# The last output projection by seven products of half-size blocks, in two units

## What is computed

```python
o = o * jax.nn.silu(z)                  # attention output, gated: 256 x 1024
x = x + gate_row * (o @ w_out_odd)      # w_out_odd: 1024 x 1024; gate_row comes from the condition
return rms_norm(x, final_g)             # 256 x 1024
```

## Time and profile before

| what | value |
|---|---|
| median of 3 runs | 1536.67 us (1536.63 to 1539.48) |
| the profiled execution | 1536.52 us, of which 1534.7 us are the span of the profile |
| TensorE busy | 1515.6 us, 99% of the span |
| VectorE, ScalarE, GpSimd busy | 1036.0, 431.0 and 12.3 us |
| granted TensorE clock, mean | 0.998 of full speed |

### The profile page before, as it was taken

How to read it: one execution, slowest core, us unless ns; L and a number is a source line. 1 busy time by engine, 2 the same in 40 slices (tenths; PEclk the granted TensorE clock), 3 DMA queues, 4 the chain that set the end, 5 groups by cost and what they waited for, 6 DMA issues and landing times.

```text
span 1534.7 us, 27707 instructions
## 1 busy us (share of the span) xinstructions
PE 1515.6 (99%) x11119; PEld 1344.5 (88%) x11119; DVE 1036.0 (68%) x1942; ACT 431.0 (28%) x925; POOL 12.3 (1%) x26
## 2 busy tenths in 40 slices
PE   8999999999999999999999999999999999999998
PEld 7998869898899999899878899799999787678887
DVE  5788886477667774678897467667775564536663
ACT  5415424012100001335423201300011365424432
POOL 1000000000000000100000000000000000000000
PEclk9999999999999999999999999999999999999999
DMA  8543453353465445344242442485454746373420
GB/s 278 185 165 111 150 153 111 111 198 131 148 237 165 153 169 178 119 163 154 101 157 92 165 142 97 146 274 165 159 179 159 245 163 220 111 289 121 141 109 28
DMA packets 176993, 243.42 MB, mean 159 GB/s; under 512 B 21438, under 2 KB 99940, under 8 KB 176868
## 3 DMA queue, kind: packets, MB, share of 16 engines
q1 hardware_dynamic: 174980, 237.98, 45.3%
q10 hardware_dynamic: 1888, 3.67, 0.7%
HBM read 240.56 MB, written 1.05 MB: 157 GB/s over the span
## 4 chain that ended last, share of the span: by engine, by line
PE 95%; DVE 2%; DMA 1%; ACT 1%; issue 0%; ACTq 0%; DVEq 0%; SPq 0%
PE psum L630 34%; PE psum L1657 27%; PE psum L1512 7%; PE psum L1312 3%; PE psum L3125 3%; PE psum L445 2%; PE psum L1571 2%; PE psum L3225 2%; PE psum L1307 2%; PE psum L3217 2%; PE psum L428 2%; PE psum L1441 1%; PE psum L1564 1%; PE psum L461 1%; PE psum L1413 1%; PE psum L1352 1%
## 5 line engine op out<-in xcount | busy, mean ns | idle before, releaser
L630 PE MATMUL psum<-hT,ring 128*128 128x256 f32 x1552 | 342.8, 380 | 0.9 <-ACT hT L3322 0.7
L630 PEld LDWEIGHTS psum<-hT,ring 128*128 128x128 f32 x1552 | 292.3, 190 | 45.4 <-issue 6.9
L630 PE MATMUL psum<-uT,ring 128*128 128x256 f32 x384 | 84.9, 380 | 0.0
L1657 PE MATMUL psum<-hT,ring 128*128 128x128 f32 x704 | 82.3, 275 | 0.0
L630 PEld LDWEIGHTS psum<-uT,ring 128*128 128x128 f32 x384 | 72.6, 190 | 10.4 <-DVE uT L1175 0.6
L1657 PEld LDWEIGHTS psum<-hT,ring 128*128 128x128 f32 x704 | 80.5, 192 | 0.0
L1938 ACT ACTIVATE SCR<-SCR 128x512 f32<-128x512 f32 x22 | 13.9, 630 | 220.2 <-DVEq L2723 220.2
L491 ACT ACTIVATE SCR<-psum,stats 128x128 f32<-128x128 f32 (+2 forms) x128 | 49.7, 405 | 26.1 <-DVE stats L526 25.3
L512 DVE TENSOR_TENSOR psum<-psum,const 128x512 f32<-128x512 f32 (+4 forms) x41 | 22.1, 559 | 43.4 <-PE psum L445 42.5
L1657 PE MATMUL psum<-G,ring 128*128 128x128 f32 x400 | 47.8, 276 | 0.0
L477 ACT ACTIVATE SCR<-psum 128x512 f32<-128x512 f32 (+2 forms) x60 | 26.3, 497 | 71.6 <-PE psum L461 71.6
(11 more groups left out here) (658 smaller groups left out, 3004.0 us busy)
## 6 DMA issues: line engine op xcount, KB each, us to landing
ring<-in_w_in SPq DMA_DIRECT2D x46, 1024.0 KB, 7.0
ring<-in_ffn_w_gate_up SPq DMA_DIRECT2D x88, 512.0 KB, 5.6
ring<-in_w_ada SPq DMA_DIRECT2D x24, 1024.0 KB, 7.7
ring<-in_ffn_w_down SPq DMA_DIRECT2D x16, 1024.0 KB, 6.0
ring<-in_w_in_odd SPq DMA_DIRECT2D x16, 1024.0 KB, 7.9
ring<-in_w_in_even SPq DMA_DIRECT2D x10, 1024.0 KB, 7.1
ring<-in_x_w_kv SPq DMA_DIRECT2D x8, 1024.0 KB, 5.9
ring<-in_ssm_w_glu SPq DMA_DIRECT2D x8, 1024.0 KB, 6.5
```

The lines of the kernel that those rows point to most:

```text
L630: ins = nc.tensor.matmul(b[0:width, n * S:n * S + S], w[k // 4][:, k % 4, c0[n]:c0[n] + width], tile(k), start=k == 0, stop=k == kt - 1)
L1657: ins = nc.tensor.matmul(banks[job][:, at:at + P], left, right, start=first, stop=last)
```

## The change

The last projection is made by seven products of blocks, in two units of 512 output channels (unit 0: tiles 0 to 3, unit 1: tiles 4 to 7). `odd_out(u, p)` does product p of unit u as 8 matmuls of 128x128. The products need token differences (four, shared by both units; VectorE, `odd_tokens`), sums of weight blocks for unit 0 (four, VectorE, `odd_weights`) and for unit 1 (four, GpSimd, the new block). The first three products fill steps 8 and 9 of the attention; the other eleven follow behind its last step in the order of `OUT_LATE`. GpSimd starts when Z1's last job is full (its sums are read no more) and VectorE has normalised the last rows. VectorE makes sum 0 and difference 0 at the head of step 8, sum 1 in step 9, the rest behind the last step.

`odd_store` combines the products in `whole` and adds two tiles at a time into `xT` (`odd_added`). ScalarE copies product 1 of each unit into `one` and squares four tiles of unit 0 and twice two of unit 1. The gains come four, two and two at a time. The sums of squares take five passes on TensorE (tiles 0 with 1 to 3 added in, 5, 7, 4, 6) where there were two.

```diff
-          8: ["part 0", "part 1"], 9: ["part 2"]}
+          8: ["part 0 1", "part 0 5"], 9: ["part 1 1"]}
...
-ODD_TILES = EVEN_TILES[0:3] + [slice(6, 7), slice(7, 8)]
+OUT_JOBS = [(0, "a"), (1, "a"), (0, "b"), (0, "c"), (0, "d"), (1, "b"), (1, "c"), (1, "d")]
+OUT_LATE = [(1, 5), (0, 2), (1, 2), (0, 6), (0, 7), (0, 4), (0, 3), (1, 6), (1, 7), (1, 4), (1, 3)]
...
-    names += [f"odd out{c}" for c in range(5)] + [f"final{n}" for n in range(4)]
+    names += [f"O{u} {job}" for u, job in OUT_JOBS] + [f"final{n}" for n in range(4)]
...
-        wide(f"odd out{n}", a["w_out_odd_2"], 512 * n, 512, f"odd out{(1, 4)[n]}")
+        wide(f"odd out{n}", a["w_out_odd_2"], 512 * n, 512, f"O{n} d")
...
+    odd_sums = [[QKr[:, 1024 * i:1024 * i + 1024].rearrange("p (k g n) -> p k g n", g=2, n=P) for i in range(4)], sums]
+    def odd_quarters(eng, u):
+        w = [ring.arrived(eng, f"odd out{u}.{h}").rearrange("p k (g m n) -> p k g m n", g=2, m=2) for h in range(2)]
+        return [[w[half][:, :, :, m_, :] for half in range(2)] for m_ in range(2)]
...
+    @block.gpsimd
+    def _(pool):
+        jobs.full(pool, f"{SEVENS[-1]} d")
+        pool.wait_ge(rows_ready, att_c.base + len(C_UNITS))
+        q, made = odd_quarters(pool, 1), odd_sums[1]
+        nc.gpsimd.tensor_tensor(made[0], q[1][0], q[1][1], ALU.add).then_inc(sig["pool_mixed"], 1)
+        pool.wait_ge(sig["pool_mixed"], 1)
+        nc.gpsimd.tensor_tensor(made[1], made[0], q[0][0], ALU.subtract).then_inc(sig["pool_mixed"], 1)
+        nc.gpsimd.tensor_tensor(made[2], q[0][0], q[1][0], ALU.subtract).then_inc(sig["pool_mixed"], 1)
+        pool.wait_ge(sig["pool_mixed"], 3)
+        nc.gpsimd.tensor_tensor(made[3], q[0][1], made[1], ALU.subtract).then_inc(sig["pool_mixed"], 1)
     @block.tensor
...
+        def odd_out(u, p):
+            job = next(x for x, made in PRODUCTS.items() if p in made)
+            i, name = PRODUCTS[job].index(p), f"O{u} {job}"
+            first = p in (1, 5) or job in "cd" and i == 0
+            if first:
+                out_banks[name] = jobs.begin(pe, name, early=p in (1, 5))
+            b = out_banks[name]
+            w = [ring.arrived(pe, f"odd out{u}.{h}") for h in range(2)]
+            if p in MIXED_OF:
+                pe.wait_ge(sig["tokens_mixed"], 4 + MIXED_OF[p] + 1)
+            if p in SUM_OF:
+                if u:
+                    pe.wait_ge(sig["pool_mixed"], SUM_OF[p] + 1)
+                else:
+                    pe.wait_ge(sig["weights_mixed"], 4 * len(SEVENS) + SUM_OF[p] + 1)
+            for g in range(2):
+                for k in range(4):
+                    if p in TOKENS_OF:
+                        half, n = TOKENS_OF[p]
+                        if g == 0:
+                            odd_tile(4 * half + k)
+                        tokens = z[:, 4 * half + k, n * P:(n + 1) * P]
+                    else:
+                        tokens = mixed[MIXED_OF[p]][:, k, :]
+                    if p in WEIGHTS_OF:
+                        m_, half = WEIGHTS_OF[p]
+                        weights = w[half][:, k, 256 * g + P * m_:256 * g + P * m_ + P]
+                    else:
+                        weights = odd_sums[u][SUM_OF[p]][:, k, g, :]
+                    at = S * i + P * g
+                    ins = nc.tensor.matmul(b[:, at:at + P], weights, tokens, start=k == 0, stop=k == 3)
+            if p in (2, 6, 4, 3):
+                close(ins)
...
                 if name.startswith("part"):
-                    out_part("odd", int(name[-1]), range(4), odd_tile)
+                    odd_out(int(name[5]), int(name[7]))
...
-        finish("odd", 4, odd_tile)
         def final(n):
...
-                pe.wait_ge(sig["gained_out"], (1, 1, 2, 2, 3, 3, 4, 5)[4 * half + i])
+                pe.wait_ge(sig["gained_out"], (1, 1, 1, 1, 3, 2, 3, 2)[4 * half + i])
...
-        for c, c0 in zip((3, 4), pair(3)):
-            transposed(f"odd out{c}", wide("odd out1"), (c0,), z, KT, (P,))
+        for u, p in OUT_LATE:
+            odd_out(u, p)
...
         b = ojobs.begin(pe, "square 3")
-        pe.wait_ge(sig["summed"], 4)
-        for k in (0, 7):
+        pe.wait_ge(sig["summed"], 3)
+        for k in (0, 5, 7, 4, 6):
...
-                pe.wait_ge(sig["squares"], 13)
+                pe.wait_ge(sig["squares"], 10 if k % 2 else 11)
...
-                                       start=k == t == 0, stop=k == 7 and t == 1)
+                                       start=k == t == 0, stop=k == 6 and t == 1)
...
         def square(n):
...
-            for c, tiles in enumerate(EVEN_TILES if n == 2 else ODD_TILES):
-                jobs.evacuated(act, f"{'even' if n == 2 else 'odd'} out{c}")
-                nc.scalar.activation(sq[:, tiles, :], xT[:, tiles, :], ACT.Square).then_inc(sig["squares"], 1)
+            if n == 2:
+                for c, tiles in enumerate(EVEN_TILES):
+                    jobs.evacuated(act, f"even out{c}")
+                    nc.scalar.activation(sq[:, tiles, :], xT[:, tiles, :], ACT.Square).then_inc(sig["squares"], 1)
+            else:
+                for u in range(2):
+                    b = jobs.full(act, f"O{u} a")
+                    if u:
+                        jobs.evacuated(act, "O0 b")
+                    else:
+                        jobs.evacuated(act, f"{SEVENS[-1]} b")
+                    nc.scalar.activation(one, b[:, 0:S], ACT.Copy).then_inc(sig["parts_copied"], 1)
+                for job, tiles in (("O0 d", slice(0, 4)), ("O1 c", slice(5, 8, 2)), ("O1 d", slice(4, 7, 2))):
+                    jobs.evacuated(act, job)
+                    nc.scalar.activation(sq[:, tiles, :], xT[:, tiles, :], ACT.Square).then_inc(sig["squares"], 1)
...
-        def final_gains(c):
-            jobs.evacuated(dve, f"odd out{c}")
-            for k in range(ODD_TILES[c].start, ODD_TILES[c].stop):
+        def final_gains(tiles):
+            for k in tiles:
...
-        def residual(prefix, layer, before, all_tiles, after=None):
+        def residual(prefix, layer, before, all_tiles):
...
-                if after:
-                    after(c)
-                if len(all_tiles) > 4 and c == 3:
-                    dve.wait_ge(sig["squares"], before + 4)
-                    link(V.tensor_tensor(sq[:, 0, :], sq[:, 0, :], sq[:, 6, :], ALU.add))
-                    dve.sem_inc(sig["summed"], 1)
...
+        def odd_weights(*which):
+            q, made = odd_quarters(dve, 0), odd_sums[0]
+            for i in which:
+                x, y, op = ((q[1][0], q[1][1], ALU.add), (made[0], q[0][0], ALU.subtract),
+                            (q[0][0], q[1][0], ALU.subtract), (q[0][1], made[1], ALU.subtract))[i]
+                link(V.tensor_tensor(made[i], x, y, op))
+                dve.sem_inc(sig["weights_mixed"], 1)
+        def odd_tokens(which):
+            t = [[z[:, 4 * half:4 * half + 4, n * P:(n + 1) * P] for n in range(2)] for half in range(2)]
+            operands = ((t[0][1], t[0][0]), (t[1][1], mixed[0]), (t[1][1], t[0][1]), (t[1][0], mixed[1]))
+            for i in which:
+                link(V.tensor_tensor(mixed[i], *operands[i], ALU.subtract))
+                dve.sem_inc(sig["tokens_mixed"], 1)
+        whole = [m["cT"][:, i].rearrange("p a b -> p (a b)").rearrange("p (n g t) -> p n g t", n=2, g=2) for i in range(2)]
+        part = [[x[:, n].rearrange("p g t -> p (g t)") for n in range(2)] for x in whole]
+        def odd_added(u, m_, what, ns=slice(0, TT)):
+            for g in range(2):
+                k = 4 * u + 2 * g + m_
+                x = xT[:, k, :].rearrange("p (n t) -> p n t", n=TT)[:, ns, :]
+                ins = V.scalar_tensor_tensor(out=x, in0=what[:, :, g, :], scalar=ada[:, 40 + k:41 + k], in1=x,
+                                             op0=ALU.mult, op1=ALU.add)
+            return ins
+        def odd_store(u, job):
+            name = f"O{u} {job}"
+            if job == "a":
+                dve.wait_ge(sig["parts_copied"], len(SEVENS) + u + 1)
+            b = jobs.full(dve, name)
+            first, second = b[:, 0:S], b[:, S:2 * S]
+            if job == "a":
+                jobs.release(V.tensor_tensor(part[0][0], one, second, ALU.add), name)
+                jobs.evacuated(dve, name)
+            elif job == "b":
+                link(V.tensor_tensor(two, one, first, ALU.add))
+                jobs.release(V.tensor_tensor(part[0][1], two, second, ALU.add), name)
+                jobs.evacuated(dve, name)
+            elif job == "c":
+                V.tensor_tensor(part[1][1], part[0][1], first, ALU.add)
+                link(V.tensor_tensor(part[1][0], two, first, ALU.add))
+                link(V.tensor_tensor(part[1][0], part[1][0], second, ALU.add))
+                jobs.release(odd_added(u, 1, whole[1]), name)
+                jobs.evacuated(dve, name)
+                if u:
+                    link(odd_added(u, 0, whole[0]))
+            else:
+                if u == 0:
```

(32 more changed lines are left out.)

## The result

The changed kernel takes 1539.55 us (median of 20 runs, 1538.33 to 1542.83) where the kernel before takes 1536.32 beside it (median of 20, 1534.89 to 1539.48): a ratio of 1.0024, 95% interval 1.0018 to 1.0030. It is slower by a quarter of a per cent. The prediction named 0.2% as the bound of no change: the ratio lies just past it, and its interval reaches to both sides. The profiled execution of after took 1539.45 us, its span 1536.4.

The account below looks back on a forecast made before the run. TensorE, busy 1515.6 of 1534.7 us, was taken as the bound; its 2.8 us gain shrinks to 0.2 through VectorE's adding (1536.3), GpSimd's turns add 1.7: 1538.0, or 1538.2 against the median. Range 1535.6 to 1541.2.

Parts of the forecast that it names:

- TensorE's products: Output projection on TensorE: 14 products of 1.786 us replace 27.6 us of products, so the stage ends 2.8 us earlier.
- VectorE's adding shrinks the gain to 0.2: Behind the last attention output: VectorE's sums of products set the end from 1515 on, leaving 0.2 of 2.8 us: 1536.3.
- rival 3: End of the projection: VectorE's chain is shorter than added up, the root at most 2.8 us earlier, 1533.7 to 1535.5; chance 0.07.
- The turn: GpSimd's sums beside VectorE's two-input SBUF instructions: they take turns, each sum of 128x1024 costing VectorE 1.75 us.
- Rival 2: GpSimd's sums beside VectorE: the turn is the whole GpSimd instruction, 2.5 us a sum, making 1541.0; chance 0.19.
- The waits on TensorE: Unit 0's product 2 waits 1.5 us for VectorE's last head store, product 7 another 0.2; all that follows 1.7 later.
- Rival 1: GpSimd's sums beside VectorE: turns fit VectorE's gaps or are under 1.3 us, spare time swallows them, 1536.3; chance 0.26.
- Rival 4: GpSimd's first add must be fetched, delaying unit 1's first product with a sum; up to 1549.7; chance 0.06.

Follow-up runs that it names:

- e1_no_sums: Changed kernel without GpSimd's four sums, unit 1's four products reading plain weights (another result): 1535.79 us, ratio to before 0.9998.
- e6_no_adds: Changed kernel without GpSimd's sums and without VectorE's adding of products, except the last two multiply-adds of O1 d (another result): 1536.70 us, one run.
- e4_later: Changed kernel with GpSimd's sums started behind VectorE's last weight sum and product 5 of unit 1 behind unit 0's last product: 1539.77 us, ratio to before 1.0019.
- e8_copies: Changed kernel with GpSimd copying four blocks of 128x1024 in place of its sums (another result): 1534.78 us, one run.
- e2_fill: Changed kernel with GpSimd filling the same four buffers, reading nothing, in place of its sums (another result): 1535.89 us, ratio to before 0.9998.
- e5_quarters_tail: Changed kernel, GpSimd's sums in 256 columns, unit 1's product 5 later, two multiply-adds moved from O1 c to O1 b, adds of squares on GpSimd: 1536.97 us, ratio 1.0009.
- e7_vector_sums: Changed kernel with all eight weight sums on VectorE, none on GpSimd, and unit 1's product 5 behind unit 0's product 2: 1538.15 us, ratio to before 1.0014.
- e9_halves: Changed kernel with each GpSimd sum made as two instructions of 512 columns: 1538.98 us, one run.
- e3: Changed kernel with each GpSimd sum made as four instructions of 256 columns: 1536.98 us, ratio to before 1.0002.
- e10: Changed kernel, GpSimd's sums in 256 columns, unit 1's product 5 behind unit 0's product 2, two multiply-adds moved from O1 c to O1 b: 1536.84 us, ratio 1.0002.

## Why the prediction was nearly right, and where it was short

The range held and the mechanism was the one predicted; the likeliest time was 1538.2 and the kernel takes 1539.55. By the ratio the side that came is slower by more than 0.2%, which had been given 0.27 against 0.70 for no change; 1539.55 itself lies just inside the bound of 1539.7 that the prediction named. By its steps:

- **TensorE's products.** Predicted 2.8 us earlier, measured 2.46: in e1_no_sums the last transposes start 27.78 us after the first product, before 30.24. A product between two others takes the predicted 1.79; where a product stands next to a group of attention outputs or transposes, or ahead of one, the stretch is 0.09 to 0.17 longer (1498.64 to 1500.52 is 1.88). Those joints were not in the sum.
- **VectorE's adding shrinks the gain to 0.2.** Right: 0.24 in e1_no_sums. From O0 c's first add to the root it was to take 13.2 us; after it is 12.73 (1517.53 to 1530.26). That is 0.5 less, and about as much was lost ahead of it: O0 c's first add starts 19.1 us after the first product in e1_no_sums (1498.64 to 1517.76), 18.5 in the prediction. That the two cancel is luck. And the reason given was only part of it. Of the 2.2 us by which the end grew (root behind the last transposes: 1.86 before, 4.08 in e1_no_sums), 0.88 go with VectorE's adds and 1.34 stay without them (e6_no_adds): that is TensorE's twelve more records of sums of squares at 0.11, of which the prediction had priced four. So rival 3 could never have given 2.8: with nearly no adding the gain is 1.1.
- **The turn.** This is the step that failed in size. I took 8 x 0.22 = 1.75 us from the add at L2083; it measured 2.10, 2.04, 1.81 and 1.37. The runs show what that row meant. In every first meeting VectorE waits the GpSimd instruction's own length, less its head start, less about 0.14: 2.35 - 0.11 - 0.14 = 2.10 for a sum, 1.04 - 0.13 - 0.14 = 0.77 for a copy, and for the row itself 0.47 - 0.10 - 0.14 = 0.23. So 0.22 was what is left of a whole instruction, with 0.24 taken off that hardly changes with the length; I multiplied that remainder by eight. Nor was the row's 0.47 a place where GpSimd "meets nothing": the add at L2083 stands beside it, and GpSimd, which had begun first, was not stretched, as the first sum of after is not (2.35 beside the gating, 2.35 undisturbed in e4_later). Rival 2 had the sum at 2.5 us. The figure in the Trainium skill, "GPSIMD Engine Reference", section "Performance versus the Vector engine", makes 2.25, an estimate; the measured 2.35 lies between the two.
- **The waits on TensorE.** Product 2 was to wait 1.5 and product 7 0.2; they waited 2.50 and 0.51, at the predicted places and for the predicted releasers. TensorE lost another 0.5 us around these waits, which the sum had not: the last transposes start 31.28 us after the first product, 27.78 in e1_no_sums. So the sums cost 3.5 us where 1.7 was predicted. Larger turns explain only part of it. The three ahead of the last head store add up to 5.95 us in place of 5.25; the fourth is shorter than predicted, and all four make 7.3 in place of 7.0. GpSimd's first sum also began 3.1 us after the first product (1494.91 to 1498.04), 2.8 in the prediction. The slope that rival 2 gave, 0.4 us of time for 0.1 of turn, makes 1538.0 + 4 x 0.35 = 1539.4 for a turn of 2.1, and the profiled execution took 1539.45. That fit is luck: the four turns average 1.83.
- **Rival 1** (no collision that matters) holds where turns are short (e8_copies, 31.84), not for the sums. **Rival 2** was the right mechanism: exclusion for a GpSimd instruction's length, here 2.1 rather than 2.5. The Trainium skill, "SBUF — State Buffer", "Who interferes with whom", states it as an exclusive lock under which the second fully blocks, not for GpSimd instructions that only write; e2_fill and e8_copies agree (1.22 and 1.99 us for the first gating, 1.22 without GpSimd in e1_no_sums). I had read L2083's row as speaking against it, since VectorE went on before the GpSimd record ended; the 0.14 us is that lead, in each of these first meetings. **Rival 4** did not come: GpSimd's first sum started 0.14 us behind the last normalised row, with no fetch to be seen. Whether one lay earlier in GpSimd's wait of 847 us is not shown.

What stays open: an order in which all of GpSimd's sums run beside adds that read PSUM, which they leave alone (e4_later), was not tried.

## What to carry over

Before work is given to an idle engine, list the instructions on the busy engine that will run beside it and ask which of them it keeps out; here each GpSimd sum cost VectorE 1.4 to 2.1 us, more than the 1.22 for which VectorE makes it itself. If the work has to go there, cut it into short instructions: VectorE's waits fell from 7.3 to 2.5 us for the same sums in quarters, and the stage from 35.35 to 32.27 (before 32.10). And where a faster product leaves a longer end, price that end on every engine: 2.46 us saved on TensorE were worth 0.24.

## What the runs showed of the hardware

- A GpSimd instruction's wait on VectorE goes by its length (0.48, 1.02, 2.10 us for 256, 512 and 1024 columns of a sum), and VectorE gets its turn between two of them.
- The gains, with one SBUF input and a scalar, are held as well: 2.16 us for four beside an add of squares on GpSimd (e5_quarters_tail), 1.14 without. Adds with one input in PSUM kept 0.42 in e4_later.
- TensorE's granted clock fell ahead of the root in two runs. In e7_vector_sums it was 1.00 up to 1526, 0.73 in the next 2 us and then 0.50 (1.2 GHz), after TensorE had waited 1.88 us with four records since the transposes; eight sums of squares took 1.86 us. In e9_halves it was 0.92 from 1528 to 1530 and then 0.50, and eight took 1.48. In e4_later a wait of 2.07 at the same place was followed by eight in 1.05 and eight in 1.07, and the clock fell about the root (0.85 from 1530 to 1532, then 0.50). What decides was not settled.
- The clock also fell some 160 us ahead of the projection, in some executions and not in others, though TensorE had waited for the same two things just before (0.76 to 0.77 and 0.94 to 0.99 us in all twelve profiles). From 1335 to 1340 it was 1.00 in after, e3, e7 and e8, whose projections start at 1494.7 to 1495.7; 0.66 to 0.71 in before, e2, e5 and e9 (1496.4 to 1497.7); 0.50 in e1, e4, e6 and e10 (1497.7 to 1498.6). That is most of what sets the starts apart: from the attention outputs at 1334.30 in after (1335.04 in e1_no_sums) to the end of the 24 records that follow, TensorE took 6.9 us in after and 9.9 in e1_no_sums. The kernel before has it too, and it lies ahead of every edit. The stretch in after and in e1_no_sums (columns as in the stretches of e7_vector_sums):

```profile
1335.00:1340.00 5.00, 5.00 (x30) 4.41 (x27) 1.23 (x6) 0.94 (x3) 0.00 (x0) 1.00 0.14 6
1335.00:1340.00 5.00, 4.96 (x20) 3.89 (x21) 1.72 (x8) 1.64 (x9) 0.00 (x0) 0.50 0.28 34
```
